# Experts in the order of their token counts, with the second expert's weights, the gathering product and the loop's order of products changed

## The reference

```
g = argmax over 4 groups of the sum of the 2 best scores; expert = the 2 best of that group
gates = their sigmoid scores, divided by their sum
act = silu(h @ w_gate[e]) * (h @ w_up[e]) * gates
out = sum over the two experts of act @ w_down[e]       # w_gate, w_up: 1024 x 512, w_down: 512 x 1024
x = x + gate2 * out; y = rmsnorm(x) * final_norm_w
```

## Time and profile before

| what | us |
|---|---|
| median of three executions | 579.46 |
| the profiled execution | 576.9 |
| its span | 575.1 |
| front, up to the sorting | 0 to 255 |
| experts, from the first gathering product to the last down product | 255 to 560 |
| the end | 560 to 575 |

### The profile page before, as it was taken

The page is one execution under the profiler, slowest core; times in us unless marked ns, Lnnn a source line. Parts: engine busy times, 40 slices in busy tenths (PEclk is TensorE's granted clock), DMA queues, the critical chain, the costliest instruction groups (busy, mean ns, idle before and its releaser), DMA issues. The chain is left out here.

```text
span 575.1 us, 8706 instructions
## 1 busy us (share of the span) xinstructions
PE 487.0 (85%) x3246; PEld 238.8 (42%) x3247; DVE 226.6 (39%) x542; ACT 146.7 (26%) x281; POOL 109.3 (19%) x185
## 2 busy tenths in 40 slices
PE   2779979999787999969799997898797798797873
PEld 1225668564686544656523332232232232232221
DVE  2689977999843105573400010100000000000086
ACT  3546873710367201420300110000000000001043
POOL 3000514888911061023000000000000000000341
PEclk9987999999888999975989999998998899898898
DMA  8990050856699920218999959399999999999732
GB/s 293 377 391 6 15 188 12 303 211 229 215 387 403 410 94 0 111 71 308 425 422 421 425 199 369 123 376 425 426 429 423 419 426 421 424 421 419 233 125 109
DMA packets 38149, 165.13 MB, mean 287 GB/s; under 512 B 2760, under 2 KB 3528, under 8 KB 32352
## 3 DMA queue, kind: packets, MB, share of 16 engines
q1 hardware_dynamic: 31408, 146.32, 64.3%
q10 hardware_dynamic: 4288, 10.33, 4.7%
q0 software_dynamic: 2416, 7.98, 3.7%
HBM read 153.28 MB, written 11.34 MB: 286 GB/s over the span
## 5 line engine op out<-in xcount | busy, mean ns | idle before, releaser
L712 PE MATMUL psum<-arena 128*64 128x512 f32 x672 | 159.6, 630 | 18.8 <-DVE arena L1516 12.8
L712 PEld LDWEIGHTS psum<-arena 128*64 128x64 f32 x672 | 52.3, 145 | 115.1 <-issue 107.1
L725 PE MATMUL psum<-arena 128*64 128x512 f32 x336 | 81.0, 626 | 17.4 <-ACTq L1044 14.4
L1521 DVE TENSOR_TENSOR arena<-arena,psum 128x256 f32<-128x256 f32 x21 | 8.8, 421 | 186.0 <-ACT arena L1017 186.0
L1771 POOL DMA_INDIRECT arena<-sorted_outputs,src_u x6 | 5.7, 955 | 277.7 <-DMA sorted_outputs<-arena 276.2
L725 PEld LDWEIGHTS psum<-arena 128*64 128x64 f32 x336 | 26.4, 144 | 65.0 <-issue 65.0
L1017 ACT ACTIVATE arena<-psum 128x256 f32<-128x256 f32 x21 | 8.1, 384 | 149.7 <-PE psum L712 149.7
L641 PE MATMUL psum<-arena 128*128 128x512 f32 x96 | 41.5, 592 | 0.0
L641 PEld LDWEIGHTS psum<-arena 128*128 128x128 f32 x96 | 18.2, 190 | 22.3 <-issue 22.0
L505 PE MATMUL psum<-arena 128*128 128x388 f32 x64 | 24.8, 537 | 1.1 <-ACT arena L880 1.1
L1033 ACT ACTIVATE arena<-psum 128x512 f32<-128x512 f32 x19 | 11.3, 597 | 49.6 <-PE psum L725 48.3
(11 more groups left out here) (315 smaller groups left out, 642.3 us busy)
## 6 DMA issues: line engine op xcount, KB each, us to landing
arena<-in_w_gate SPq DMA_DIRECT2D x16, 2048.0 KB, 16.2
arena<-in_w_up SPq DMA_DIRECT2D x16, 2048.0 KB, 21.1
arena<-in_w_down SPq DMA_DIRECT2D x16, 2048.0 KB, 18.0
arena<-in_w_mod SPq DMA_DIRECT2D x12, 2048.0 KB, 15.2
arena<-in_w_in SPq DMA_DIRECT2D x3, 2048.0 KB, 19.5
sorted_outputs<-arena ACTq DMA_DIRECT2D x38, 128.0 KB, 7.5
arena<-in_w_out SPq DMA_DIRECT2D x2, 2048.0 KB, 14.5
arena<-modulation_rows ACTq DMA_DIRECT2D x3, 1024.0 KB, 10.6
```

What stands on the lines that cost most here:

```text
L712: last = mm(bank[0][HALF * t:HALF * t + HALF, :], xs[:, k, :], gu[:, :, k, t * 256:t * 256 + 256], start=(k == 0), stop=(k == KD - 1))
L725: last = mm(bank[4][HALF * h:HALF * h + HALF, :], hiddenT[:, s * P + t * HALF:s * P + t * HALF + HALF], dn[:, 2 * t + s, h * 512:h * 512 + ...
```

## The change

The number of tokens decides the order of the experts. DVE forms a key for each expert, 32 times its count plus a fixed rank, in which expert 0 has 65536 and expert 1 has 32768, so that these two stay first; it compares all keys with all (`larger`, 16x16), and gets each expert's start row, its place, and the expert at each place (`exp_i`). SP reads `exp_i` and loads the weights of the expert at a place; counts and offsets are by place.

Blocks 13 and 14 of w_mod are loaded and used earlier: 13 while PE turns the state-space matrices, 14 after the state-space output. So slots 0 and 1 are free early, and the loads of expert 1 now stand ahead of the six of `hsr`. The gate weight of the third expert is loaded when the first product and the one-hot matrices are done, its other two after the sorted rows are transposed.

The first 64 tokens are now picked with `places` as the weights: 12 matmuls of 64x256 in two column halves, held by ACT and DVE, transposed by four more and staged. All other sorted rows but the first tile are transposed inside expert 0, after its second pass. `xs` has two sides, so the tokens of an expert's second pass are staged before its first pass is multiplied. The loop has one order of products: the gate and up products of the next expert always stand before the last down product of this one.

```diff
-        place = (0, 1, 3, 4, 0, 1, 0, 7, 8, 1, 7, 8, 0, 1, 0)
-        NPRE = 15
+        place = (0, 1, 3, 4, 0, 1, 0, 7, 8, 1, 7, 8, 0, 0, 1)
+        loaded = (0, 1, 2, 3, 4, 5, 13, 6, 7, 8, 9, 10, 11, 12, 14)
...
+            prologue_unit(13)
+            sp.wait_ge(S("unit_used"), 6)
             prologue_unit(6)
             sp.wait_ge(S("params_done"), 1)
...
             prologue_unit(8)
-            for i in range(9, 13):
-                sp.wait_ge(S("unit_used"), i - 3)
+            for i in (9, 10, 11, 12, 14):
+                sp.wait_ge(S("unit_used"), {9: 7, 10: 8, 11: 9, 12: 10, 14: 11}[i])
                 prologue_unit(i)
...
-                sp.wait_ge(S("unit_used"), 11 + h)
+                sp.wait_ge(S("unit_used"), 12 + h)
                 sp.dma_start(wout[h], w_out[:, :, h * 512:h * 512 + 512]).then_inc(S("wout_in"), 16)
-            for i in range(13, 15):
-                sp.wait_ge(S("unit_used"), (10, 13)[i - 13])
-                prologue_unit(i)
...
-                    sp.dma_start(gu[:, i], w[:, e, :, :]).then_inc(S(f"gu_in{j}"), 16)
+                    sp.dma_start(gu[:, i:i + 1], w[:, bass.ds(e, 1), :, :]).then_inc(S(f"gu_in{j}"), 16)
...
-            def reload(j, e):
-
-                sp.wait_ge(S("gated"), (e - 2) * PASSES)
+                sp.dma_start(expert_weights(j)[1].unsqueeze(1), wd[:, bass.ds(e, 1), :, :]).then_inc(S(f"dn_in{j}"), 16)
+
+            def expert_at(place):
+
+                return sp.value_load(exp_i[0:1, place:place + 1], min_val=0, max_val=NE - 1)
+
+            def reload(j, place):
+
+                e = expert_at(place)
+                sp.wait_ge(S("gated"), (place - 2) * PASSES)
                 load_gate_up(j, e)
-                sp.wait_ge(S("downed"), (e - 2) * PASSES + 1)
+                sp.wait_ge(S("downed"), (place - 2) * PASSES + 1)
                 load_down(j, e)
...
-            for t in range(6):
-                if t == 0:
-                    sp.wait_ge(S("tok_sent"), 16 * 6)
-                sp.dma_start(hsr[:, t, :], hsd[t * P:(t + 1) * P, :]).then_inc(S(f"hs_in{t}"), 16)
             sp.wait_ge(S("unit_used"), 15)
             load_gate_up(1, 1)
             sp.wait_ge(S("yt_done"), 4)
-            sp.wait_ge(S("modd_in5"), 16)
+            sp.wait_ge(S("modd_in5"), 32)
             load_down(1, 1)
+            sp.wait_ge(S("tok_sent"), 16 * 6)
+            for t in range(6):
+                sp.dma_start(hsr[:, t, :], hsd[t * P:(t + 1) * P, :]).then_inc(S(f"hs_in{t}"), 16)
+            sp.wait_ge(S("first_ready"), 1)
+            sp.wait_ge(S("onehots_done"), 1)
+            sp.wait_ge(S("pad_sent"), 48)
+            sp.wait_ge(S("int_done"), 1)
+            third = expert_at(2)
+            sp.dma_start(expert_weights(2)[0][:, 0:1], wg[:, bass.ds(third, 1), :, :]).then_inc(S("gu_in2"), 16)
             sp.wait_ge(S("hs_ready"), 12)
-            sp.wait_ge(S("pad_sent"), 48)
-            load_gate_up(2, 2)
-            load_down(2, 2)
+            sp.dma_start(expert_weights(2)[0][:, 1:2], wu[:, bass.ds(third, 1), :, :]).then_inc(S("gu_in2"), 16)
+            load_down(2, third)
             for e in range(SETS, NE):
...
+            pe.wait_ge(S("bt_copied_a"), 7)
+            modulation(13, 4).then_inc(S("mrow_ready"), 1)
             pe.wait_ge(S("u_done_a"), 1)
...
             pe.wait_ge(S("ws_copied"), 1)
+            modulation(14, 4).then_inc(S("mrow_ready"), 1)
             for t in range(NT):
...
-            modulation(13, 6).then_inc(S("mrow_ready"), 1)
             route(1)
             h2_columns(2, 2)
             route(2).then_inc(S("logits_ready"), 1)
-            pe.wait_ge(S("mrow_done"), 7)
-            modulation(14, 6).then_inc(S("mrow_ready"), 1)
             pe.wait_ge(S("mk_done"), 1)
             pe.wait_ge(S("tri_done"), 1)
             mm(bank[3][:, 0:NT * NE + NE + 1], tri[:, :], chosen_row, start=True, stop=False)
...
-            def expert_rest(j, e, use):
+            def other_sorted_columns():
+                pe.wait_ge(S("late_copied"), 2)
+                for t in range(1, 6):
+                    sorted_columns(t)
+                pe.wait_ge(S("hs_copied_a"), 6)
...
                 with pe.If(n > HALF):
-                    gate_up(j, turn(1, e), None)
+                    gate_up(j, turn(1, e), None, 1)
                     down(j, use + 1, turn(1, e), turn(0, e))
                     transposes(turn(1, e))
+                    if is_first:
+                        other_sorted_columns()
...
             pe.sem_inc(S("downed"), 1)
             pe.wait_ge(S("placed"), 1)
-            for k in range(KD):
-                for t in range(NT):
-                    last = mm(bank[2][:, k * HALF:k * HALF + HALF],
-                              h2[:, t, :].rearrange("p (q k) -> p k q", k=KD)[:, k, :], places[:, t, :],
-                              start=(t == 0), stop=(t == NT - 1))
+            for t in range(NT):
+                for b in range(2):
+                    for h in range(2):
+                        k = 4 * h + 2 * b
+                        last = mm(bank[2 + 3 * b][HALF * h:HALF * h + HALF, 0:256], places[:, t, :],
+                                  h2[:, t, :].rearrange("p (q k) -> p k q", k=KD)[:, k:k + 2, :],
+                                  start=(t == 0), stop=(t == NT - 1))
+            last.then_inc(S("first_ready"), 1)
+            pe.wait_ge(S("first_held"), 2)
+            for kk in range(4):
+                last = tr(bank[1 - kk // 2][:, kk % 2 * P:kk % 2 * P + P], first_rows[:, kk * P:kk * P + P], ident[:, :])
             last.then_inc(S("first_sorted"), 1)
+            pe.wait_ge(S("first_staged"), 1)
...
-            for t in range(1, 6):
-                sorted_columns(t)
             pe.wait_ge(S("int_done"), 1)
-            pe.wait_ge(S("hs_copied_a"), 6)
-            pe.wait_ge(S("hs_copied_v"), 6)
-            with pe.Fori(0, 5) as i:
+
+            def three_experts(i):
                 for j in range(SETS):
                     e = i * SETS + j
-                    expert_rest(j, e, i)
-                    if j == 2:
-                        down(j, i + 1, turn(PASSES, e), turn(PASSES - 1, e))
+                    expert_rest(j, e, i, is_first=(isinstance(e, int) and e == 0))
                     gate_up((j + 1) % SETS, turn(0, e + 1), i + (j + 1) // SETS + 1)
-                    if j < 2:
-                        down(j, i + 1, turn(PASSES, e), turn(PASSES - 1, e))
+                    down(j, i + 1, turn(PASSES, e), turn(PASSES - 1, e))
                     transposes(turn(0, e + 1))
+
+            three_experts(0)
+            with pe.Fori(1, 5) as i:
...
+            v(stt(key, bank[3][:, NT * NE + 1:NT * NE + 1 + NE], 32.0, prio[:, :], ALU.mult, ALU.add))
+            d(cp(counted, bank[3][:, NT * NE + 1:NT * NE + 1 + NE]))
+            v(tt(larger, key.unsqueeze(1).broadcast_to(square), key.unsqueeze(2).broadcast_to(square), ALU.is_gt))
+            v(tt(product, larger, counted.unsqueeze(1).broadcast_to(square), ALU.mult))
+            v(V_.tensor_reduce(starts, product, AX.X, ALU.add))
             v(tt(r2, bank[3][:, 0:NT * NE].rearrange("p (t e) -> p t e", t=NT),
-                 off.unsqueeze(1).broadcast_to([P, NT, NE]), ALU.add))
+                 starts.unsqueeze(1).broadcast_to([P, NT, NE]), ALU.add))
...
+            off, cnt, place = sel[:, 1, :], row[:, 1:NE + 1], r2[:, 0, :]
+            ids = count_row[:, 0:NE]
+            v(V_.tensor_reduce(place, larger, AX.X, ALU.add))
+            v(tt(larger, place.unsqueeze(1).broadcast_to(square), ids.unsqueeze(2).broadcast_to(square), ALU.is_equal))
+            v(tt(product, larger, ids.unsqueeze(1).broadcast_to(square), ALU.mult))
+            v(V_.tensor_reduce(r2[:, 1, :], product, AX.X, ALU.add))
+            d(cp(exp_i[:, :], r2[:, 1, :]))
+            v(tt(product, larger, counted.unsqueeze(1).broadcast_to(square), ALU.mult))
+            d(V_.memset(row[:, 0:1], 0.0))
+            v(V_.tensor_reduce(cnt, product, AX.X, ALU.add))
+            v(V_.tensor_tensor_scan(off, ones[:, 0:NE], row[:, 0:NE], 0.0, ALU.mult, ALU.add))
             d(cp(n_i[:, :], cnt))
             d(cp(off_i[:, :], off))
...
             dve.wait_ge(S("first_sorted"), 1)
-            cp(xs[:, :, :], bank[2][:, :].rearrange("p (k j) -> p k j", k=KD)).then_inc(S("x_staged"), 1)
+            cp(xs[:, 0].rearrange("p (h k) j -> p h k j", h=2)[:, :, 2:4, :],
+               bank[0][:, 0:256].rearrange("p (k h j) -> p h k j", k=2, h=2)).then_inc(S("x_staged"), 1)
+            d(ts(r2[:, 0, :], cnt, float(HALF), None, ALU.is_gt))
+            d(ts(r2[:, 1, :], cnt, float(P), None, ALU.is_gt))
+            v(ts(r2[:, 2, :], cnt, float(P + HALF), 3.0, ALU.is_gt, ALU.mult))
+            v(tt(r2[:, 0, :], r2[:, 0, :], r2[:, 1, :], ALU.add))
+            v(tt(r2[:, 0, :], r2[:, 0, :], r2[:, 2, :], ALU.add))
+            v(stt(r2[:, 1, :], r2[:, 0, :], float(HALF), off, ALU.mult, ALU.add))
```

(18 more changed lines are left out.)

204 lines of the change are left out of this document (122 added, 82 removed).

## The result

The changed kernel takes 590.2 us (median of four runs, 585.5 to 593.0) against 581.0 for the kernel before in the same session: a ratio of 1.015, 95% interval 1.011 to 1.020. Measured once more later (four executions), it took 589.2, ratio 1.016 (1.009 to 1.023). So the change makes the kernel 1.5% slower. I had forecast no change, 581 us, and 587 as the upper end; both were too low.

A forecast was written before the change was run, and what follows sets the result against it. PE was taken to set the pace until about 372, the loads from there on. The terms summed to +1.7 us, 578.6 against the profiled 576.9, or 581.2 on the median; forecast 581, range 572.3 to 587.

The forecast's parts named there:

- the routing: Before the picking product: 0.95 us saved without modulation 13, 1.5 more for DVE's operations; picking starts at 256.4 instead of 255.49.
- The front: Stages before the routing: modulation 13 moved there adds 0.4 us through to the end, modulation 14 and expert 1's early weights 0.
- Expert 0 to expert 1: Expert 0's second pass at 275.6, then 12.6, 5.0, 2.1 and 0.45 us: expert 1 at 295.9 instead of 300.87.
- The picking product: Picking the first 64 tokens: 5.0 us instead of 11.68, from 2.7 at full and 5.3 at half clock.
- My first rival: PE's clock high in the early stage: picking product 2.7, gates about 7 us; 7.4 us go, 573.8; chance 0.28.
- The loads and the last places: Place 7's loads issued at 387, then no break; last gate and up land at 525.0; PE waits from place 10.
- The end: After the last gates: last full output at 537.3, gather 4.7 us later at 542.0; dropping the last second pass gives 0.3.
- the rival of the late write: At the end, the last write takes up to 7.5 us instead of 3.1: +4.4, 585.6; chance 0.13.
- The order: Expert 15's second pass at place 4: load breaks grow to 37 us from 18, eating 14.9 of expert 1's weights.
- the early stage is longer: Before the last load break, transposes waiting for ACT, DVE's chain and unrolled code add 4 to 6 us: 585 to 587; chance 0.07.

The follow-up runs named there:

- The clock runs: Unread identity matmuls in PE's routing waits: on the changed kernel 601.0 us; fewer, with spread order, transposes ahead of the loop and row loads first, 572.8 us.

## Why the prediction was wrong, by its steps

The span was forecast at 576.8 and came out at 588.3 and 587.4, 11.5 and 10.6 us later. By the milestones, the way from expert 0's second pass to expert 1's gates has 4.8 and 3.6 of that, and the routing 3.7 and 3.9. The front has +1.6 and -1.6, all other steps together 1.4 and 4.7.

**Expert 0 to expert 1 failed.** I had the gates of expert 1 20.3 us behind the second pass of expert 0; they came 25.1 and 23.9 behind it. I counted a wait of PE of 3 us, VectorE's way to the staging, and that way did take 3.2. But PE stood for 7.76 and 7.62 us. The term that I had at nothing is the 4.6 and 4.5 behind the staging, of which about 3.3 are gone when no weights are loaded. I had costed every instruction that moved, and nothing that passes through the transfer engines beside the weights, at a moment when the change itself fills them: up and down of place 2 and the next gates and ups are issued just as the gap begins. Putting the transposes back gives 7 to 9 us in two kernels; part of that is that up of place 2 is then issued at 283.0 instead of 298.8.

**Routing failed by a term that I had at nothing.** I counted 0.55 more, -0.95 for modulation 13 and +1.5 for VectorE; from the output projection to the picking product it became 4.2 and 4.5 us more (61.7 before, 65.9 and 66.1 now). Both counted terms held: from the first routing product to the second it takes 1.15 and 1.20 us less, and VectorE's operations between the ranks and the picking product add 1.4 (5.2 instead of 3.8). What was missing are the products at half clock, the second and third routing product and the columns between them (3.25, 1.95 and 3.60 instead of 1.96, 1.07 and 1.96, so 3.8 us more): the granted clock from 236 to 248 was 0.97 and then 0.71 until 256 before; now it is 0.74 from 238 to 248 and then 0.50. The clock runs show that filling PE's waits keeps the clock up, so that the modulation had done this is likely, and that the filling costs as much as it gives.

**The picking product** was counted at 5.0 for a reason that is wrong. It took 5.77 at 0.58 and 5.73 at 1.00, and 2.81 at 1.00 without the strides, so at full clock it is the strided read that binds. That 5.0 came near is luck. My first rival, a high clock with the product at 2.7, was impossible in this term; the gates at full clock, its other half, came partly true (7.09 for the first) without making the kernel faster. From the picking product to the second pass I had 19.2; it took 19.7 in both.

**The front** held within what executions differ by: +2.0 in one profile, -1.2 in the other, against +0.4.

**The loads and the last places** held. From place 2's gates to the issue for place 7 I had 77.9; measured 77.9 and 78.0. From there to the last gates 138.0; measured 139.2 and 139.0. PE waits for the loads from place 10 on. The loads went at 419 GB/s; the rule in the Trainium skill (DMA: Bandwidth & Descriptors, Where 436 GB/s comes from), by which about 358 bind, is not seen here either.

**The end** held in the first profile: 51.1 us from the last gates, where I had 51.8. In the second it took 54.4, with those gates at 10.02 instead of 7.09. In the first the gather started at 551.70, 3.9 us behind the last full output's down product (547.8); I had 4.7. The last write landed in 2.23, so the rival of the late write fell:

```profile
549.20 2.23 DMA sorted_outputs<-arena
551.43 0.27 issue
551.70 1.00 POOL arena L1865
```

**The order.** I said that a second pass at place 4 eats what expert 1's early weights gave, and left it there as a break even. It is a loss of 6 us against the order of numbers, and the one change of it that pays, long experts between short ones, was not among my rivals. The rival that came nearest, "the early stage is longer", had 0.07. It named the place, but its 4 to 6 us were about half of the 9 by which the time was off, and of its causes VectorE's chain took what I had counted, and the unrolled code by itself didn't make this gap. It deserved the weight that I gave to the high clock: three additions met in one stage (VectorE's chain, moved transposes, new code), and my sum had no term for what they do to each other.

**Open.** No run has expert 1's earlier weights or the moved modulations by themselves, so what each gives or costs in time isn't known.

## What to carry to other kernels

With a few sets of buffers and loads that just keep pace, the order of unequal work matters by its neighbours: long pieces in a row stop the queue of loads, and here that time wasn't won back; a piece of two passes between short ones didn't stop it, one of three did once. Sort by size only to alternate. Before work is moved out of an engine's waits, ask what else it did there: it may hold the clock up. And before a burst of loads is moved, look whether an engine stands still for no reason that the profile shows just then; that it waits for its code there is the likely reading, not a shown one.

## What the runs showed of the hardware that I had not expected

- A product of 12 matmuls of 256 columns in fp32 takes 5.7 to 5.8 us with a moving operand read at a stride of eight elements, at a granted clock of 1.00 as at 0.58 to 0.68; with the elements one behind the other 2.81 at 1.00 and 4.80 at 0.61.
- PE stands still for 3.8 to 7.9 us between two products, for longer than the staging that the next one needs, ahead of the gates of different places in the kernels (1, 2, 3, 4 and 6). Ahead of expert 1 it goes on 2.5 to 2.7 us behind the start of an instruction packet on q8, with the transfer engines full or idle; at the other places 2.9 to 3.4 us behind one. With no weights being loaded the gap there was 3.1 to 3.3 us shorter (4.48 instead of 7.62 and 7.76).
- Two executions of the same program start their output projection 3.2 us apart (195.8 and 192.6); a front can't be judged by one profile.
- POOL's two operations on 2048 elements beside VectorE stretched single sums of 0.69 to as much as 2.7 us, with no effect on the start of the columns of h2.
